# A fused four-layer kernel: the first block's projection in another column order, values token-major, embeddings taken by ScalarE

## What is computed

```
u  = rmsnorm(h, e_norm) @ e_w_in                 # 2048 x 6144
qa, fa, ia, za, xb, zb = six slices of 1024
ya = hgrn2(qa, fa, ia, lb)                       # gated linear recurrence, 8 heads
ya = head_rmsnorm(ya, a_norm) * silu(za)
xc = causal_conv(xb)                             # 4 taps
r, i = sigmoid(blockwise xc @ w_r + b), sigmoid(blockwise xc @ w_i + b)
a  = exp(-8 r softplus(-lambda));  s_t = a_t s_(t-1) + sqrt(1 - a_t^2) i_t xc_t
yb = s * silu(zb)
h  = h + [ya, yb] @ e_w_out
pl = rmsnorm(p @ ple_w, ple_norm)                # 256 -> 2048
h  = h + sigmoid(h @ ple_gate_w) * pl
```

## Time and profile before

| | |
|---|---|
| timed runs | 2367.03, 2374.01, 2374.76 us (median 2374.01) |
| the profiled execution | 2365.19 us, span 2363.0 us |
| busy share of the span | TensorE 93%, weight load 80%, GpSimd 75%, VectorE 54%, ScalarE 52% |
| chain that ended last | TensorE 44%, GpSimd 23%, issue 15%, VectorE 14%, ScalarE 2% |

### The profile page before, as it was taken

The page is one execution under the profiler, slowest core; times in us unless marked ns, Lnnn a source line. Parts: engine busy times, 40 slices in busy tenths (PEclk is TensorE's granted clock), DMA queues, the critical chain, the costliest instruction groups (busy, mean ns, idle before and its releaser), DMA issues.

```text
span 2363.0 us, 39021 instructions
## 1 busy us (share of the span) xinstructions
PE 2204.8 (93%) x12256; PEld 1895.4 (80%) x12256; DVE 1269.3 (54%) x1902; ACT 1232.0 (52%) x2195; POOL 1783.1 (75%) x1390
## 2 busy tenths in 40 slices
PE   7998886799999999989998989999999999988997
PEld 6887775688888888868887867888888888876886
DVE  4356687624564137774256666452854565368712
ACT  5463354456544445555565436444655544466654
POOL 6984456799898977668997946876789877745695
PEclk9999998999999999999999989999999999999998
DMA  7653232466556654435665633555466665533464
GB/s 262 205 174 111 90 107 71 141 189 190 179 179 181 191 172 135 133 112 171 186 189 167 193 105 119 185 174 163 141 187 190 196 188 177 187 108 109 138 185 134
DMA packets 211099, 378.96 MB, mean 160 GB/s; under 512 B 23440, under 2 KB 34320, under 8 KB 210832
## 3 DMA queue, kind: packets, MB, share of 16 engines
q1 hardware_dynamic: 205056, 363.95, 50.2%
q10 hardware_dynamic: 5904, 13.23, 1.6%
HBM read 374.99 MB, written 2.10 MB: 160 GB/s over the span
## 4 chain that ended last, share of the span: by engine, by line
PE 44%; POOL 23%; issue 15%; DVE 14%; ACT 2%; POOLq 1%; DVEq 0%; ACTq 0%
PE ps L448 25%; POOL w_lo L401 23%; PE ps L449 12%; PE ps L530 1%; PE ps L441 1%; PE ps L442 1%; PE ps L443 1%; PE ps L698 1%; DVE ps L1364 1%; DVE tb L1363 1%; ACT w_hi L808 1%; DVE w L1538 1%; DVE ob L1607 1%; DVE w L1369 1%; DVE w L1452 1%
## 5 line engine op out<-in xcount | busy, mean ns | idle before, releaser
L401 POOL TENSOR_TENSOR w_lo<-raw,w_hi 128x512 fp32r<-128x512 f32 (+1 forms) x1386 | 1782.9, 1307 | 559.4 <-ACT w_hi L808 513.8
L808 ACT ACTIVATE w_hi<-raw 128x512 fp32r<-128x512 f32 (+1 forms) x1420 | 857.2, 619 | 780.7 <-PE ps L449 716.3
L448 PE MATMUL ps<-xa,w_hi 128*128 128x512 f32 x2960 | 1066.9, 404 | 51.7 <-POOL w_lo L401 30.0
L449 PE MATMUL ps<-xa,w_lo 128*128 128x256 f32 x2960 | 833.3, 282 | 0.0
L448 PE MATMUL ps<-xb,w_hi 128*128 128x512 f32 x2160 | 763.7, 398 | 1.8 <-POOL w_lo L401 1.5
L448 PEld LDWEIGHTS ps<-xa,w_hi 128*128 128x128 f32 x2960 | 562.8, 190 | 194.2 <-POOL w_lo L401 25.8
L449 PE MATMUL ps<-xb,w_lo 128*128 128x256 f32 x2160 | 604.7, 280 | 0.0
L449 PEld LDWEIGHTS ps<-xa,w_lo 128*128 128x128 f32 x2960 | 565.7, 191 | 0.9
L448 PEld LDWEIGHTS ps<-xb,w_hi 128*128 128x128 f32 x2160 | 405.1, 188 | 100.3 <-issue 3.6
L449 PEld LDWEIGHTS ps<-xb,w_lo 128*128 128x128 f32 x2160 | 407.8, 189 | 0.5
L1363 DVE TENSOR_SCALAR tb<-ps 128x512 f32<-128x512 f32 (+1 forms) x124 | 85.2, 687 | 365.2 <-PE ps L449 363.6
(11 more groups left out here) (308 smaller groups left out, 2061.3 us busy)
## 6 DMA issues: line engine op xcount, KB each, us to landing
raw<-w_gate_dram SPq DMA_DIRECT2D x128, 256.0 KB, 3.0
raw<-w_ogz_dram SPq DMA_DIRECT2D x128, 256.0 KB, 3.0
raw<-w_odin_dram SPq DMA_DIRECT2D x128, 256.0 KB, 3.0
raw<-w_evmoba_dram SPq DMA_DIRECT2D x112, 256.0 KB, 3.0
raw<-w_ein_dram SPq DMA_DIRECT2D x96, 256.0 KB, 3.1
raw<-w_evout_dram SPq DMA_DIRECT2D x80, 256.0 KB, 2.9
raw<-w_odgate_dram SPq DMA_DIRECT2D x72, 256.0 KB, 3.0
raw<-w_ein_zx_dram SPq DMA_DIRECT2D x64, 256.0 KB, 3.0
```

Source lines behind the costliest of these rows:

```text
L401: nc.gpsimd.tensor_tensor(w_lo[:, slot, 0:n], raw[:, at, 0:n], w_hi[:, slot, 0:n].bitcast(F32), SUB).then_inc(lo_pool, 1)
L448: mm(ps[:, bank + b, :], w_hi[:, slot, at], x[:, x0 + k, :], start=(k == 0), stop=False)
L449: ins = mm(ps[:, bank + b, 0:T], w_lo[:, slot, at], x[:, x0 + k, 0:T], start=False, stop=(k == st.blocks - 1))
L808: af(w_hi[:, slot, 0:n], raw[:, at, 0:n], ACT.Copy).then_inc(act_rounded, 1)
```

## The change

The columns of `e_w_in` are put in another order, and the first layer's stages with them. `ein` is now xb, q, f; `einv` the values, 2 pairs of 16 units with 512 columns; `einz` zb and za, 8 pairs. The rows of `e_w_out` are swapped to match (yb first).

```diff
-        ("ein_zx", "xa", 16, 8, 2),
-        ("ein_zb", "xa", 16, 4, 2),
+        ("einv", "xa", 16, 2, 2, 512),
+        ("einz", "xa", 16, 8, 2),
...
-            units = [2, 3, 3, 3, 3, 3, 3, 2, 2][slot % 9]
+            units = [3, 4, 4, 4, 4, 4, 4, 3, 2][slot % 9]
```

```diff
@@ product
+                        if st.narrow:
+                            to = ps[:, bank + b, 0:T]
+                            mm(to, w_hi[:, slot, at], x[:, x0 + k, 0:T], start=(k == 0), stop=False)
+                            mm(to, w_hi[:, slot, at], x[:, x0 + k, T:2 * T], start=False, stop=False)
+                            ins = mm(to, w_lo[:, slot, at], x[:, x0 + k, 0:T], start=False, stop=(k == st.blocks - 1))
+                            continue
@@ scalar, value stage
+                if (p, q) == (0, 1):
+                    act.wait_ge(pair_out, STORED["ein"] + 8)
+                    af(sg, w[:, 0:8, :], ACT.Sigmoid).then_inc(hg_sig, 1)
+                if (p, q) == (0, 3):
+                    act.wait_ge(lr_fix, 1)
+                    af(ob[:, 24:32, :], ob[:, 24:32, :], ACT.Sqrt).then_inc(lr_root, 1)
...
+                if (p, q) == (0, 7):
+                    act.wait_ge(hg_q, 1)
+                    af(sg, w[:, 8:16, :], ACT.Sigmoid).then_inc(hg_sig, 1)
@@ scalar, decay
+                act.wait_ge(hg_diff, 8 * g + level)
+                if 8 * g + level > 1:
+                    act.wait_ge(hg_lv_in, 8 * g + level - 1)
...
+                af(grown, d, ACT.Exp).then_inc(hg_exp, 1)
@@ scalar, after the slots
+                af(r, ps[:, 4 + c, :], ACT.Ln).then_inc(hn_std, 1)
+                for u in range(6 + 2 * c, 8 + 2 * c):
+                    rounded(ple0, u // 2, u % 2)
+                keep_ple(0, c)
...
+            for c in range(4):
+                keep_ple(0, 4 + c)
+                for q in range(2 * c, 2 * c + 2):
+                    rounded(ST["eout"], 0, q)
+                act.wait_ge(hn_y, 2 + c)
+                af(xb[:, 8 + 2 * c:10 + 2 * c, 0:T], ps[:, 4 + c, :].rearrange("p (a b) -> p a b", b=T),
+                   ACT.Copy).then_inc(y_hi, 1)
@@ vector, behind ein
+            dve.wait_ge(lr_th, 16)
+            step(tt(t1, r_, r_, MUL))
+            stt(th, t1, 1.0, th, ADD, MUL).then_inc(lr_fix, 1)
             streamed("p0", 0, 0, None, xs, 0)
...
+            tt(q, q, ob[:, 32:40, :], MUL).then_inc(hg_q, 1)
+            dve.wait_ge(lr_root, 1)
+            step(tt(ig, ig, th, MUL))
+            for n in range(8):
+                step.post(nc.vector.tensor_tensor_scan(y_lru[:, n, :], r_[:, n, :], ig[:, n, :], 0.0, MUL, ADD))
+            step.wait()
             dve.wait_ge(hg_sig, 2)
             tt(kk, kk, wide(oml, 8), MUL).then_inc(hg_qk, 1)
+            values(ST["einv"], 0)
```

More of the change, by code:

```diff
@@ L86, in __init__ @@
         self.unit0, self.pair0 = unit0, pair0
+        self.narrow = self.name[:3] == "ple"
         self.turn = 2 if self.upp % 4 == 0 else 4
@@ L941, in _ @@
             stage("ein", first=0, count=2, peel=2, behind=x_norm)
-            stage("ein", first=2, count=8, peel=2, behind=mem_norm)
-            stage("ein", first=8, count=10, peel=2, behind=mem_norm)
-            stage("ein", first=10, peel=2, behind=lambda p, par, q: (
-                root("mem", RS_MEM) if p == 11 and q == 5 else None))
-            stream("p0", 0, 0)
-            zx, zb = ST["ein_zx"], ST["ein_zb"]
-            for q in range(4):
-                rounded(zx, 0, q)
-            act.wait_ge(pair_out, STORED["ein"] + 12)
@@ L1063, in gate_norm @@
                             round_h(None, so.name, 7, 1, None)
+                        if q == 5:
+                            root(ple.name, RS_PLE)
                     else:
@@ L1159, in _ @@
                 af(w[:, 41, :], w[:, 42, :], ACT.Sqrt).then_inc(ml_std, 1)
-            def head7_behind(p, par, q):
-                if p == 1 and q == 1:
-                    head_gates(7)
-            tail(1, "first", "ev_norm", head7_behind)
+            tail(1, "first", "ev_norm")
             act.wait_ge(x_ready, XR["p1"] + 1)
@@ L1620, in _ @@
                 differences(1)
+                if g == 0:
+                    values(ST["einv"], 1)
                 masked(0)
```

562 lines of the change are left out of this document (290 added, 272 removed).

## The result

| | before | after |
|---|---|---|
| median of four runs | 2370.5 us | 2335.0 us (2330.2 to 2336.7) |
| the profiled execution | 2365.2 us, span 2363.0 | 2336.7 us, span 2334.6 |
| ratio | | 0.985, 95% interval 0.982 to 0.989 |

What follows compares the result with a forecast made beforehand. TensorE bounds the first projection; behind it, chains of VectorE and ScalarE with TensorE waiting. -47.8 up to the output projection, -2 for squares, -7.3 for ple pairs: -57.1, so 2313 us from 2370.5; range 2290 to 2342, eight in ten.

Steps and rivals of the forecast that it cites:

- the slots did not go in series: Rival, level slots: ScalarE's rounding waits behind an exponential that waits for VectorE's scaling; 69 us more, 2382, chance 0.06.
- Part 1: First projection: sixteen recurrent gate products add 5.4 us, convolutions and activations nothing; it ends at 160.5 us.
- Part 2: Value stage, values token-major: 43.6 us for 32 units plus three delays; level 0 starts at 218.1, 33.6 us behind.
- step (c): Value stage: VectorE's 32 log decay scans (15.9 us) lie beside pair two, whose slower units cost 2 us: 23.8.
- (a): Value stage: ScalarE's square root behind the fourth value unit waits for VectorE, so TensorE idles 6.5 us.
- Part 3: Level slots with all gate pairs: 141.4 us against 136.2, ending at 359.5 us, 38.8 us behind.
- Part 4: After the slots: 32.9 us instead of 119.5; output projection starts at 392.4 instead of 440.2, 47.8 us ahead.
- Part 5: Output projections: the sum over squares of the embedding leaves the second output pair; -2 us.
- Part 6: Second layer's ple pairs: the second TensorE wait goes with its slow restart, narrow products cost 1 us; -7.3 us.
- the cheaper of the two prices of the narrow products: Second layer's ple pairs: three narrow products for one cell cost 3 x 0.121 us, against at most 3 x 0.17.
- The first one: Rival, mainly value stage: GpSimd becomes the bound as its operations grow beside VectorE's SBUF work; 2328 us, chance 0.20.
- The rule of the Trainium skill: VectorE with two SBUF inputs and GpSimd exclude each other for whole instructions; units beside wide operations at about 3.1 us.

Runs made afterwards that it cites:

- The experiment: Changed kernel with the scans' second input in PSUM, and GpSimd's subtraction cut to 64 of 512 columns in the level slots alone: 2312.6 us in one run.
- the first kernel with everything together: Changed kernel plus PSUM scan inputs, scans ahead of the first value pair's taking, later root and sigmoids, spread fetches, early copies: 2316.6 us.
- the last: Changed kernel plus scan inputs and square in PSUM, keys scaled by eight operations, later root and sigmoids, spread fetches, early copies; value pair before scans: 2312.8 us.

## Why the prediction was right, and where it was off

**Right in kind and inside the range** (2290 to 2342), in its upper half: 22 us above the value, 28.7 in the span (the mean of the four runs before is 2370.2, not 2370.5; the value stays 2313). The moves did what was said, the slots did not go in series, and the kernel became faster by trading 119.5 us of chains for 36.8. Some of the nearness is luck: without what GpSimd costs VectorE, the value stage (53.6 us) and the slots (136.0) would have come 4 and 5 us under their forecasts, so other terms of these sums were too large, and what was left out is larger than the differences in the table.

**Part 1** (+4.0). From 40 us on TensorE waited for nothing over 1 us in the projection, so convolutions, sigmoids and the rest were hidden as forecast. The four pairs with gate products are 6.5 us longer than four of the kernel before, where 5.4 was charged. What I left out are ScalarE's issues: the two gate weights were put behind a row that was eight long already, and the rounding behind it waits 6.8 us instead of 3.7. TensorE's two waits there were 1.18 and 2.25 us before and are 4.29 and 0.90 now, and the lower clock behind the long one costs 1.7 more; the pair that holds them is 3.1 us longer. I counted only the instructions that compute. The size varies: the stall was 4.3 us in the changed kernel and 2.3 to 3.3 in seven that have the same order there.

**Part 2** (+8.6), above all step (c). The 15.9 us for 32 scans were taken over as a price; they are 5.9 us of scans and 10 of waiting for ten subtractions, and where sixteen fall beside them they become 22.5. I charged the contention to GpSimd alone, and too much (1.53 us a unit), and never to VectorE, in whose row it stood. For (a) the wait is 4.99 against 6.5, but I put nothing for the lower clock behind it, and the first pair ended 4 us late. Taking the wait out there gained only 0.8 us, as the run with the later root shows, since waits beside wide operations took its place; taking the contention off the scans gained the whole miss (57.3 us against 57.6).

**Part 3** (+9.7). The same step: two differences at 0.6 each were taken from slots of three units, where nearly all of them do run free (0.69 us); beside denser subtractions they take up to 3 us together. The experiment puts 14 us on GpSimd.

**Part 4** (+3.9). ScalarE's queue was added up as if it never waited; it waits 5.5 us for TensorE. The 1.7 us for the start at half clock were counted ahead of the first product, but lie behind it. The seventh `ple` copy as the release of the output projection was right, the row at 418.64 names it (L1063).

**Part 5** (-0.7). The sum's wait is gone from both output projections. The second layer's is 2.2 us shorter, the first layer's only 0.45, since it starts at the lower clock (first product 0.79 us). **Part 6** was right in its sum, and the cheaper of the two prices of the narrow products holds: the three of a cell start 0.12 us apart. The stage of the second layer in the changed kernel:

```profile
1028.52 0.58 PE L462 MATMUL ps<-xs,w_hi 128*128 128x256 f32 x1 [5.58 <-DVE oa L1422]
...
1041.48 0.47 PE L466 MATMUL ps<-xa,w_hi 128*128 128x512 f32 x1 [0.16 <-POOL w_lo L401]
```

13.0 us from the stage's first product to that of the next, against 20.3 before (1050.91 to 1071.16), with only the first of the two waits left.

**The rivals.** The first one (GpSimd becomes the bound, 2328) came nearest in time, for the right pair of engines and the wrong victim: beside wide operations the units do go at 3.28 us (its 3.1), but only three of the 32, and nine more at 1.64 beside the recurrence; most of the price is paid by VectorE. GpSimd costs the value stage 12.6 us (66.2 against 53.6 with short subtractions), and 8.9 of them are gone once the scans read from PSUM (57.3). The rule of the Trainium skill that I had set aside with "the neighbours don't show it in full" was shown by those neighbours: the row of 18.73 us holds two subtractions of 2.96 and 3.33 us beside wide products, and ten with one scan held up beside each.

## What to carry to other kernels

A duration read beside another engine's work is a price for that neighbourhood only; before it is moved, ask what it shares with whom and how many of the other's instructions will fall beside it, and charge both sides. An operand of a long chain of small VectorE operations that lies in PSUM takes the chain out of GpSimd's way (the scans took 16.6 us less here, for one memset; the kernel 11.6 us less, with the recurrence's input). A wait that is covered now is worth its size again when its cover goes: try such an edit once more after the larger one.

## What the runs showed of the hardware

- A VectorE operation with two inputs in SBUF loses about 1.0 us to a GpSimd subtraction of 512 columns that falls beside it, however short it is itself: 64-column scans follow each other every 0.18 us alone (5.90 / 32) and every 1.25 beside subtractions, 256-column scans 0.59 (4.73 / 8) and 1.64 (13.13 / 8), and a 2048-wide product takes 2.29 and 3.35.
- GpSimd loses more the longer VectorE's operation is: a subtraction takes 1.28 us alone, 1.30 beside 64-column scans, 1.67 beside 256-column ones and 3.3 beside a 2048-wide product. The 4.54 us of the row at 166.83 are one of 1.28 and one of 3.31.
- Copies and scalings from SBUF to SBUF lose as much (1.48 us instead of 0.41 for a copy of 512 columns).
- The issue of one and the same fetch took ScalarE's queue 0.33 us alone and 2.31 us as the fifth of ten, and 0.45 in that same place in the kernel with short subtractions, where the seventh took 1.85. Why one issue is the long one stays open.
- Up to the slots of the changed kernel TensorE's granted clock was at its lower level, 1.2 GHz, at the end of the waits of 4.29, 4.99 and 8.12 us and for the products behind them, and not at those of 1.6 us. Behind a wait of 2.2 us at the start it fell in the first kernel with everything together (39.7 to 43.1 us) and not in the last.
- Single edits worth 1 to 3 us in the trace were within the scatter of the runs (2330.2 to 2336.7 us for the changed kernel); only together did they show, 2312.8 us against the 2323.4 of the PSUM scans alone.
